# The end of each RWKV head pair: one term of two sums is added by matmuls on TensorE, and the results are copied out by ScalarE

## The reference, cut to what matters

```python
def rwkv7_step(state, inp):
    r, w, k, v, kk, a = inp
    sa = jnp.einsum('...vk,...k->...v', state, -kk)
    state = (state * w[..., None, :]
             + sa[..., :, None] * (kk * a)[..., None, :]
             + v[..., :, None] * k[..., None, :])
    y = jnp.einsum('...vk,...k->...v', state, r)
    return state, y
```

## Time and profile before

| | us |
|---|---|
| median of 3 runs | 1885.8 (1882.3 to 1887.44) |
| the profiled execution | 1885.95 |
| its span | 1884.1 |
| PE busy | 1764.3 (94%) |
| DVE busy | 988.4 (52%) |
| ACT busy | 766.9 (41%) |

### The profile page before, as it was taken

The page is one execution under the profiler, slowest core; times in us unless marked ns, Lnnn a source line. Parts: engine busy times, 40 slices in busy tenths (PEclk is TensorE's granted clock), DMA queues, the critical chain, the costliest instruction groups (busy, mean ns, idle before and its releaser), DMA issues.

```text
span 1884.1 us, 32250 instructions
## 1 busy us (share of the span) xinstructions
PE 1764.3 (94%) x14281; PEld 1449.2 (77%) x14281; DVE 988.4 (52%) x1353; ACT 766.9 (41%) x1158; POOL 100.3 (5%) x79
## 2 busy tenths in 40 slices
PE   6997888888998999999998999989899999999999
PEld 5876777767778788888887886558777878888887
DVE  5476665476434456534654255984524355643652
ACT  4243444334554334413433234773555244422431
POOL 1001221000000000000000022010000000000000
PEclk9999999989999999999998999999999999999999
DMA  7210000033330222333222321003322223232222
GB/s 236 79 45 2 4 4 5 4 135 122 134 134 23 67 90 90 100 103 110 90 68 95 106 90 67 1 1 112 103 77 90 68 67 109 100 105 90 89 81 76
DMA packets 96453, 149.41 MB, mean 79 GB/s; under 512 B 3479, under 2 KB 50170, under 8 KB 96314
## 3 DMA queue, kind: packets, MB, share of 16 engines
q1 hardware_dynamic: 94727, 142.29, 23.1%
q0 software_dynamic: 1296, 4.95, 0.8%
q10 hardware_dynamic: 291, 0.12, 0.0%
HBM read 145.25 MB, written 2.10 MB: 78 GB/s over the span
## 4 chain that ended last, share of the span: by engine, by line
PE 82%; DVE 10%; ACT 4%; issue 3%; DMA 0%; POOL 0%; DVEq 0%; ACTq 0%; POOLq 0%; SPq 0%
PE PS L369 69%; DVE SS L1532 1%; PE PS L945 1%; PE PS L1330 1%; PE PS L931 1%; PE PS L495 1%; PE PS L1304 1%; PE PS L972 1%; PE PS L964 1%; DVE LOS L444 1%; DVE YQ L1276 1%; ACT EX L1343 1%; PE PS L854 1%; ACT SS L1513 1%; PE PS L1462 1%
## 5 line engine op out<-in xcount | busy, mean ns | idle before, releaser
L338 DVE TENSOR_TENSOR WLO<-WRAW,WHI 128x2048 fp32r<-128x2048 f32 (+1 forms) x132 | 296.7, 2251 | 449.1 <-ACT WHI L330 449.0
L330 ACT ACTIVATE WHI<-WRAW 128x2048 fp32r<-128x2048 f32 (+1 forms) x132 | 248.3, 1881 | 477.2 <-PE PS L369 450.8
L369 PE MATMUL PS<-HIS,WHI 128*128 128x512 f32 x856 | 333.9, 390 | 1.5 <-DVE SM L1694 1.5
L369 PE MATMUL PS<-HIS,WLO 128*128 128x512 f32 x856 | 333.1, 389 | 0.0
L369 PE MATMUL PS<-LOS,WHI 128*128 128x512 f32 x856 | 333.1, 389 | 0.0
L369 PE MATMUL PS<-WHI,HIS 128*128 128x512 f32 x608 | 238.8, 393 | 11.1 <-DVE LOS L444 4.0
L369 PE MATMUL PS<-WLO,HIS 128*128 128x512 f32 x608 | 237.8, 391 | 0.0
L369 PE MATMUL PS<-WHI,LOS 128*128 128x512 f32 x608 | 237.8, 391 | 0.0
L369 PEld LDWEIGHTS PS<-HIS,WHI 128*128 128x128 f32 x856 | 160.7, 188 | 35.4 <-DVE SM L1694 1.7
L369 PEld LDWEIGHTS PS<-LOS,WHI 128*128 128x128 f32 x856 | 160.7, 188 | 33.4 <-issue 0.2
L369 PEld LDWEIGHTS PS<-HIS,WLO 128*128 128x128 f32 x856 | 160.7, 188 | 33.2
(11 more groups left out here) (280 smaller groups left out, 2465.6 us busy)
## 6 DMA issues: line engine op xcount, KB each, us to landing
WRAW<-ffn_w_up SPq DMA_DIRECT2D x88, 512.0 KB, 4.7
WRAW<-ffn_w_down SPq DMA_DIRECT2D x20, 1024.0 KB, 5.1
WRAW<-cross_wkv SPq DMA_DIRECT2D x16, 1024.0 KB, 5.1
WRAW<-diff_w_in SPq DMA_DIRECT2D x12, 1024.0 KB, 5.1
WRAW<-ab_w_in SPq DMA_DIRECT2D x10, 1024.0 KB, 5.4
WRAW<-cross_wq SPq DMA_DIRECT2D x8, 1024.0 KB, 5.2
WRAW<-cross_wo SPq DMA_DIRECT2D x8, 1024.0 KB, 5.1
X<-x SPq DMA_DIRECT2D x8, 512.0 KB, 8.3
```

Source lines behind the costliest of these rows:

```text
L330: A.e.activation(part(WHI[i % 3], i), part(WRAW[i % 2], i), ACT.Copy).then_inc(S("w_hi"), 1)
L338: V.e.tensor_tensor(part(WLO[i % 3], i), part(WRAW[i % 2], i), part(WHI[i % 3], i).bitcast(F32), ALU.subtract).then_inc(S("w_lo"), 1)
L369: mm = e.matmul(o, l, r, start=(si == 0 and kk == 0 and q == 0), stop=(si == len(steps) - 1 and kk == nk - 1 and q == 2))
```

## The change

Rho and the unit matrix are no longer added by DVE. Before VK, two matmuls (one for each of the banks 4 and 5) with the 128x128 unit matrix as stationary and rho as moving operand, 512 columns each, write rho into the banks, and the R products accumulate onto it. Before P, two like them write the unit matrix (`ident2`, spread over the columns) into banks 0 and 1, and the P products accumulate. ACT copies R to `RT` and P to `PT`, two instructions each; `tail_dve` is gone. PE's wait for the last chain step of the pair before (c_yfree) stands ahead of VK now, and ACT's wait for c_y ahead of the copy of R.

```diff
+        def base(b, x, r):
+            e.matmul(PS[:, b + x, :].rearrange("p (d t i) -> p d t i", d=2, t=NT), ident, r, start=True, stop=False)
+
+        if j > 0:
+            e.wait_ge(S("c_yfree"), j * STEPS)
+        for x in range(2):
+            base(4, x, AR[j % 2][:, :, 1, :].rearrange("p d (t x i) -> p d t x i", t=NT, x=2)[:, :, :, x, :])
         tail(6, 0, 0, v, gkr, "bank", "")
         tail(6, 0, 1, v, gkr, "", "")
-        if j > 0:
-            e.wait_ge(S("c_yfree"), j * STEPS)
         for d in range(2):
             e.wait_ge(S("p_wuc"), 2 * j + d + 1)
-            mm = tail(4, d * 256, d, w, gbr, "each", "each")
+            mm = tail(4, d * 256, d, w, gbr, "", "bank" if d else "")
         mm.then_inc(S("p_r"), 1)
         tail(6, 0, 0, uu, gbr, "", "")
         tail(6, 0, 1, uu, gbr, "", "bank").then_inc(S("p_y"), 1)
-        tail(0, 0, 0, w, bp, "each", "each")
-        tail(0, 256, 1, w, bp, "each", "each").then_inc(S("p_p"), 1)
+        for x in range(2):
+            base(0, x, rk("ident2").unsqueeze(1).unsqueeze(1).to_broadcast([P, 2, NT, HD]))
+        tail(0, 0, 0, w, bp, "", "")
+        tail(0, 256, 1, w, bp, "", "bank").then_inc(S("p_p"), 1)
...
+        e.wait_ge(S("p_r"), j + 1)
+        if j > 0:
+            e.wait_ge(S("c_y"), j * STEPS)
+        for d in range(2):
+            i = e.activation(RT[:, d, :].rearrange("p (t x i) -> p t x i", t=NT, x=2),
+                             banks2(4, d * 256, 256).rearrange("p x (t i) -> p t x i", i=CH), ACT.Copy)
+        i.then_inc(S("p_rfree"), 1)
         e.wait_ge(S("p_y"), j + 1)
         e.activation(YL[:, j, :].rearrange("p (t x i) -> p t x i", t=NT, x=2),
                      banks2(6, 0, 256).rearrange("p x (t i) -> p t x i", i=CH), ACT.Copy).then_inc(S("p_yfree"), 1)
+        e.wait_ge(S("p_p"), j + 1)
+        for d in range(2):
+            i = e.activation(PT[:, d, :, :].rearrange("p (t x) v -> p t x v", x=2),
+                             banks2(0, d * 256, 256).rearrange("p x (t v) -> p t x v", v=HD), ACT.Copy)
+        i.then_inc(S("p_pfree"), 1)
         e.wait_ge(S("p_q"), j + 1)
-        if j > 0:
-            e.wait_ge(S("c_y"), j * STEPS)
...
-    def tail_dve(V, j):
...
-        tail_dve(V, j)
```

## The result

| | before | changed |
|---|---|---|
| median, first comparison | 1885.4 us (4 runs) | 1896.17 us (1895.46 to 1896.68, 4 runs) |
| ratio, 95% interval | | 1.0058 (1.0042 to 1.0073) |
| second comparison (e0) | 1886.9 us (17 runs) | 1898.22 us (5 runs); 1.0055 (1.0043 to 1.0067) |
| span of the profiled execution | 1884.1 us | 1894.7 us |

The change makes the kernel slower, by 10.4 to 10.9 us when the two ratios are multiplied by 1887 us. The forecast was 1893.7, 7.8 us over the profiled execution, in a range of 1888.5 to 1900.

The account below looks back on a forecast made before the run. The prediction took PE's stream and its instruction-issue holes in the four tails as the bound. Tail terms of +2.1, +2.4, +1.0 and +2.3 summed to 7.8 us over 1885.95, giving 1893.7 us, range 1888.5 to 1900.

Parts of the forecast that it names:

- The path is PE's stream, DVE's work is covered: In the four tails PE's stream and issue holes set the time; removing DVE's 10.3 us of additions is worth nothing.
- Price of the matmuls, 1.92 us for two, 15.4 in all: Four new PE matmuls per tail, priced from L882: 3.84 us a tail, the bound from above.
- The holes are instruction blocks, 128 matmul records apart, and take in what is put ahead of them: PE's issue holes in the tails, 14.2 us in all, are waits for instruction blocks and can absorb new matmul time.
- The four tails: +2.1, +2.4, +1.0, +2.3: Forecast growth in us of the tails of pairs 0 to 3, worked out border by border; sum 7.8 us.
- The decay as last wait of pair 3: Pair 3's first chain step waits for DVE's decay, not ACT's copy of Q, starting at 385.9 or 386.0 instead of 383.65.
- Between the tails the borders shift too; I take nothing, and 1 us to either side.: In the levels between tails, borders shift by up to 24 records; priced at nothing, 1 us either side.
- the sign of being wrong that the prediction named: The prediction called itself wrong if, among other signs, the levels between the tails changed by more than 1 us.
- Rival A: Tails: holes absorb none of the new matmuls' time; +15.4 us, 1901.3 us; chance 0.12.
- rival B: Tails 0, 1 and 3: sequencer runs further ahead, more is absorbed; +1.2 to +5.6, about 1889.5 us; chance 0.25.
- rival C: DVE's 10.3 us of relief counts for masks and levels; -2.5 us, or -9.1 with holes filled; chance 0.04.

Follow-up runs that it names:

- e0: The changed kernel itself, unedited, run again beside the kernel before on the same chip: 1898.22 us, ratio 1.0055.
- copies only: Kernel before with ACT copying R and P out, no DVE sums and no new matmuls; rho and unit matrix missing from the result: ratio 0.9989, -2.1 us.
- the pad: 32 small PE products ahead of pair 0, moving all borders by 64 records: ratio 1.0009 on the kernel before, 1.0053 on the changed one.
- the halves: Changed kernel with only rho on PE, or only the unit matrix, the other sum staying with DVE: 7.5 and -0.6 us over before.
- the cut columns: Changed kernel with rho's two matmuls, or the unit matrix's, cut from 512 to 64 columns: 1.9 and 7.4 us over before.
- short fill: Kernel before with two short 64x64 products repeated ahead of VK and two ahead of P, 8 PE records more per tail: ratio 1.0018, 3.4 us over.

## Why the prediction held, and which terms were off

The time lay inside the range and the sign was right; the size was forecast as 7.8 us and measured as 10.4 to 10.9.

- *The path is PE's stream, DVE's work is covered.* Shown: 10.3 us off DVE, no gain (copies only: -2.1, interval to 0.2), and DVE waits 11.90 us for GA in the changed kernel.
- *Price of the matmuls, 1.92 us for two, 15.4 in all.* Shown by PE's busy time, 53.8 to 69.2 us in the tails. The strided read of rho costs nothing more than L882's straight one.
- *The holes are instruction blocks, 128 matmul records apart, and take in what is put ahead of them.* The spacing and the tie to the count are shown by the pad, which moved the holes by its 64 records. That they take matmul time in is shown by the halves, 7.5 against -0.6 us, and by the cut columns, 8.5 against 3.0. The Trainium skill (Runtime: NRT & Kernel Launch, section Instruction fetch mechanics) has the cost of a border as mostly hidden. These tails disagree: 8.2 us of matmul time went into holes that by that rule would not be there.
- *The four tails: +2.1, +2.4, +1.0, +2.3.* The profiles shown have +2.0, +2.1, +0.6, +2.6. In sum 7.3 against 7.8. The second profile of the changed kernel has 81.3, and 7.3 is also what the means over profiles without a fallen clock give (all but one tail of the kernel before at 1.00, that one at 0.98). That the single values agree so well is partly luck, since the same stream's tails differ by 1.2 us in sum even so, and by 3 us with the clock. The decay as last wait of pair 3 came as forecast.
- *"Between the tails the borders shift too; I take nothing, and 1 us to either side."* This is the term that was mis-sized, and the sign of being wrong that the prediction named (levels changed by more than 1 us) came true: 4.8 us in one profile, 2.4 in the means. The short fill costs 3.4 us (1.1 to 5.7) with little more than records. I had worked out border by border where the holes fall in the tails, and not done so for the levels, which have nearly twice as many borders (about 34 against 19, at 4317 and 2394 records). Not all of the 2.4 us are the borders', though: by the estimate above some 1.5 are the clock, which the prediction did not look at.
- Rival A (nothing absorbed, +15.4) falls by the tails; rival B (+1.2 to +5.6) by the measured ratio; rival C (DVE's relief counts) by the copies alone.

What stays open: how the rest of the levels' growth comes about in single borders, and whether the change brings the falls of the clock. The profile's 3.3 us in pair 2 was not repeated in the second profile, and moving all borders by 64 records did not show an effect on the time clear of noise. In the levels, the seven profiles of kernels with eight more records a tail have eleven falls, one or two each, and none in the tails; the three of the kernel before's stream have one in the levels and four in the tails. So where the clock falls differs, but the number for each profile is about the same, and the runs don't show that the change costs anything by it.

## What to carry to other kernels

Where PE runs long strings of small matmuls, look for holes that wait for no engine and count the records between them: if the count is constant, the instruction stream is the limit there. A few dozen small products put where PE waits anyway test it: the holes must move by their count. Then PE time placed right ahead of such a border is nearly free, PE time elsewhere is paid in full, and what helps is to order the stream so that the products which another engine waits for come first. Take two or three profiles before explaining a difference of 2 or 3 us between stages, and read the granted clock of each stage first: the sum of one stage varied by that much from one execution to the next, and of the 3.2 us between the tails of two profiles of the kernel before 2.9 were a clock at half for some 3 us, twice.

## What the runs showed of the hardware that was not expected

With an unchanged PE stream, three profiled executions had tails of 72.8, 74.0 and 76.0 us and levels of 136.0, 138.9 and 137.0 us. The granted clock was 0.92 in two tails of the slowest and 0.96 in the longest levels; each such fall to 0.50, some 3 us long, made PE busy 1.2 to 1.4 us longer. The falls in the levels of pair 1 came within 1.4 us of the end of a wait of 2.0 to 2.2 us, but the same wait passed without one in two of the three executions. The holes of the block borders stand at the same record each time and differ in length, as the 1.22 us at 246.18 shows, which is 0.17 in the other two. Two such matmuls of 512 columns cost 1.9 us between small ones ahead of VK, ahead of P and in level 4 (210.19 to 212.10, 215.06 to 216.97, 205.13 to 207.04).
